# First mixer of a two-network kernel: a third input group takes half of its features early, the recurrence runs two pieces later, and two tables are written in the first feed-forward part

## The reference, cut to what matters

```python
mod = silu(c) @ w_ada + b_ada                  # (2048) @ (2048 x 12288)
sh1, sc1, gt1, sh2, sc2, gt2 = split(mod, 6)
h = rmsnorm(x, g_mix) * (1 + sc1) + sh1
z = h @ w_in                                   # pool | q | k | v | f | x | y
y = concat([pool_mixer(zp), forgetting_attention(zq, zk, zv, zf),
            rg_lru_branch(zx, zy)])
x = x + gt1 * (y @ w_out)
h = rmsnorm(x, g_ffn) * (1 + sc2) + sh2
x = x + gt2 * conv_glu_ffn(h)                  # gate, up, down
```

## Time and profile before

| | |
|---|---|
| median of 3 runs | 3325.72 us |
| profiled execution | 3335.25 us, span 3333.6 us |
| mean granted TensorE clock | 0.976 of full |
| busy share of the span | PE 97%, DVE 67%, ACT 43%, POOL 5% |
| mean DMA rate | 204 GB/s |
| chain that ended last | PE 86%, DVE 7%, DMA 3% |
| first mixer, p = 0 starts | 76.87 us |
| first matmul of quarter 2 (p = 4) | 134.82 us |
| FF1, p = 55 starts | 524.95 us |

### The profile page before, as it was taken

How to read it: one execution, slowest core, us unless ns; L and a number is a source line. 1 busy time by engine, 2 the same in 40 slices (tenths; PEclk the granted TensorE clock), 3 DMA queues, 4 the chain that set the end, 5 groups by cost and what they waited for, 6 DMA issues and landing times.

```text
span 3333.6 us, 62992 instructions
## 1 busy us (share of the span) xinstructions
PE 3221.1 (97%) x27070; PEld 3147.8 (94%) x27070; DVE 2223.1 (67%) x2257; ACT 1420.1 (43%) x1384; POOL 157.7 (5%) x292
## 2 busy tenths in 40 slices
PE   5999979999999999999999999999999999999998
PEld 5988879999999999989999999999988999999998
DVE  5788877766666677677665565567678755555555
ACT  3243334444444444555434433434455443443333
POOL 2111100000000100011000000000011000000000
PEclk7899999999999999999999999999999999999999
DMA  9788776766666745455555555555444555556553
GB/s 385 283 306 314 286 275 222 238 205 202 221 206 202 220 164 159 136 159 166 190 197 189 191 197 190 191 197 168 151 140 157 185 193 197 189 191 197 191 191 137
DMA packets 320747, 681.66 MB, mean 204 GB/s; under 512 B 14768, under 2 KB 21620, under 8 KB 320164
## 3 DMA queue, kind: packets, MB, share of 16 engines
q1 hardware_dynamic: 286272, 562.74, 51.1%
q0 software_dynamic: 31232, 109.07, 9.0%
q10 hardware_dynamic: 3108, 7.89, 0.6%
HBM read 677.47 MB, written 7.94 MB: 206 GB/s over the span
## 4 chain that ended last, share of the span: by engine, by line
PE 86%; DVE 7%; DMA 3%; issue 2%; ACT 1%; POOL 0%; ACTq 0%; DVEq 0%; POOLq 0%; SPq 0%
PE G L695 53%; PE Dn L695 33%; DVE ada_acc L1393 1%; DVE w_lo L1266 1%; PE Dn L698 1%; DMA ada_raw<-in_w_ada 1%; DMA raw<-in_w_in 1%; DMA zT<-in_w_ada 1%; DMA raw<-in_w_out 1%; DVE sq L1317 1%; ACT w_hi L2223 1%; DVE sq L1993 0%; DMA ada_x<-in_w_ada 0%; PE G L698 0%; DVE sq L1333 0%
## 5 line engine op out<-in xcount | busy, mean ns | idle before, releaser
L2223 ACT CAST w_hi<-raw 128x2048 fp32r<-128x2048 f32 (+2 forms) x536 | 1017.5, 1900 | 1418.3 <-DMA raw<-in_w_down 425.6
L1266 DVE TENSOR_TENSOR w_lo<-raw,w_hi 128x2048 fp32r<-128x2048 f32 (+2 forms) x536 | 1218.8, 2274 | 565.1 <-ACT w_hi L2223 564.2
L695 PE MATMUL G<-h_hi,w_hi 128*128 128x256 f32 x5632 | 1579.5, 280 | 13.6 <-DVE w_lo L1266 9.4
L695 PE MATMUL G<-h_lo,w_hi 128*128 128x256 f32 x5632 | 1568.2, 278 | 0.0
L695 PE MATMUL G<-h_hi,w_lo 128*128 128x256 f32 x5632 | 1567.8, 278 | 0.0
L695 PEld LDWEIGHTS G<-h_hi,w_hi 128*128 128x128 f32 x5632 | 1067.7, 190 | 28.6 <-issue 24.4
L695 PEld LDWEIGHTS G<-h_lo,w_hi 128*128 128x128 f32 x5632 | 1067.6, 190 | 0.3
L695 PEld LDWEIGHTS G<-h_hi,w_lo 128*128 128x128 f32 x5632 | 1067.5, 190 | 0.0
L695 PE MATMUL Dn<-act_hi,w_hi 128*128 128x256 f32 x2752 | 763.2, 277 | 7.4 <-DVE act_lo L1811 7.4
L695 PE MATMUL Dn<-act_hi,w_lo 128*128 128x256 f32 x2752 | 762.6, 277 | 0.0
L695 PE MATMUL Dn<-act_lo,w_hi 128*128 128x256 f32 x2752 | 762.5, 277 | 0.0
(11 more groups left out here) (273 smaller groups left out, 1737.4 us busy)
## 6 DMA issues: line engine op xcount, KB each, us to landing
raw<-in_w_up SPq DMA_DIRECT2D x128, 1024.0 KB, 5.4
raw<-in_w_down SPq DMA_DIRECT2D x128, 1024.0 KB, 4.9
raw<-in_w_in SPq DMA_DIRECT2D x88, 1024.0 KB, 5.2
ada_raw<-in_w_ada POOLq DMA_DIRECT2D x120, 512.0 KB, 6.7
raw<-in_w_ffn_gate SPq DMA_DIRECT2D x44, 1024.0 KB, 5.1
raw<-in_w_ffn_up SPq DMA_DIRECT2D x44, 1024.0 KB, 5.2
raw<-in_w_ffn_down SPq DMA_DIRECT2D x44, 1024.0 KB, 5.0
raw<-in_w_o SPq DMA_DIRECT2D x32, 1024.0 KB, 5.0
```

Source lines behind the costliest of these rows:

```text
L695: return nc.tensor.matmul(o, lhsT, rhs, start=start, stop=stop, skip_group_check=True)
L1266: v.tensor_tensor(w_lo[j][:, 0:m], raw[j][:, 0:PIECE_K * n], w_hi[j][:, 0:m], ALU.subtract).then_inc(lo_done, 1)
L2223: s.copy(w_hi[j][:, 0:PIECE_K * n], raw[j][:, 0:PIECE_K * n]).then_inc(hi_done, 1)
```

## The change

A half-filled third group: quarters 0 and 1 of group 2 (the pooling input) become p = 4 and 5, ahead of quarters 2 and 3 of all three groups at p = 6 to 11. Group 2 is gathered in Dn[0] instead of G[0], with a semaphore of its own. The results of the four early blocks of the modulation move to ADA_OUT (two of them to PT). The direct tiles of the last early block are 7, 10, 13 and 15 in place of 2, 5, 8 and 11, and run behind p = 5 in place of p = 3; the third block is closed behind p = 4 and read by DVE there (`second_scale`). The hooks of the small mixers move by two pieces (the convolution by one), the distribution of the 96 later tiles is new, and the temporaries move to the values' tiles of zT. `replicate` is issued by ACT behind pieces 8 to 15 of FF1.

```diff
-ORDER1 = [(0, 0), (0, 1), (1, 0), (1, 1), (0, 2), (0, 3), (1, 2), (1, 3)] + [(g, j) for g in range(2, 9) for j in range(4)]
+HALF1 = [0, 1, 2]
+ORDER1 = [(g, j) for g in HALF1 for j in (0, 1)] \
+    + [(g, j) for g in range(9) for j in ((2, 3) if g in HALF1 else range(4))]
+HALF_AT = 2 * len(HALF1)
+USE1 = {0: (0, 0), 1: (1, 0), 3: (0, 1), 4: (1, 1), 5: (0, 2), 6: (1, 2), 7: (0, 3), 8: (1, 3)}
-ADA_AT = [0, 0, 0, 0, 3, 0, 2, 2, 1, 0, 1, 2, 2, 2, 3, 2, 2, 3, 2, 3, 0, 2, 0, 1, 4, 3, 3, 2, 3, 2,
-          4, 3, 2, 2, 1, 4, 3, 4, 4, 1, 2, 0, 1, 3, 1, 2, 2, 1, 3, 1, 2, 0]
+ADA_AT = [0, 0, 0, 0, 0, 0, 3, 3, 2, 1, 2, 1, 2, 2, 3, 2, 2, 1, 3, 1, 2, 2, 3, 1, 1, 2, 2, 2, 3, 2,
+          2, 1, 3, 2, 3, 2, 1, 3, 2, 3, 2, 3, 2, 3, 2, 3, 2, 3, 2, 2, 2, 0]
-ADA_PE = [[], [3, 6, 9, 12, 15], [3, 8, 13], [2, 5, 8, 11]]
+ADA_PE = [[], [3, 6, 9, 12, 15], [3, 8, 13], [7, 10, 13, 15]]
...
+        ADA_OUT = [Dn[0][:, 0, :], Dn[0][:, 2, :], PT[:, 0, :], PT[:, 1, :]]
+        def group_buf(g):
+            return Dn[0] if g == 2 else G[USE1[g][0]]
...
-            hook(3, ada_total, 2)
+            hook(4, ada_total, 2)
             for t in ADA_PE[3]:
-                hook(3, ada_direct, 3, t)
-            hook(3, ada_total, 3)
+                hook(5, ada_direct, 3, t)
+            hook(5, ada_total, 3)
...
-                hook(11 + b, lru_gates, b)
-            hook(23, pool_map)
+                hook(13 + b, lru_gates, b)
+            hook(25, pool_map)
...
-            hook(2, ada_late, 37, 41)
-            hook(3, second_half)
+            hook(2, ada_late, 37, 40)
+            hook(3, ada_late, 40, 43)
+            hook(4, second_scale)
+            hook(4, ada_late, 43, 46)
+            hook(5, second_half)
...
-            for p, k in ((8, 2), (9, 1), (10, 0)):
+            for p, k in ((9, 2), (10, 1), (11, 0)):
                 hook(p, conv, k)
...
-            hook(22, pool_1)
-            hook(23, pool_2)
+            hook(24, pool_1)
+            hook(25, pool_2)
...
             for q in (2, 3):
-                hook(3, x_hat_hi, q)
+                hook(5, x_hat_hi, q)
             for g in range(len(IN1)):
-                hook(LAST1[g] + 1, evac1, g)
+                hook(LAST1[g] + (0 if g == 0 else 1), evac1, g)
...
-            for n in range(REP):
-                hook(40 + n, replicate, n)
...
+                    if n >= 16 - REP:
+                        replicate(n - 16 + REP)
```

More of the change, by code:

```diff
@@ L795, in ada_direct @@
                     pe.wait_ge(silu_c, 1)
-                    if i >= 2:
-                        pe.wait_ge(mod_ready, i - 1)
+                    if i == 3:
+                        pe.wait_ge(mod_ready, 3)
                 pe.wait_ge(ada_loaded[slot], 16 * count)
                 for j in range(8):
-                    x = mm(ada_out(i)[:, j:j + 1], ada_buf(slot)[:, j * P:(j + 1) * P], c_sil[:, t:t + 1],
+                    x = mm(ADA_OUT[i][:, j:j + 1], ada_buf(slot)[:, j * P:(j + 1) * P], c_sil[:, t:t + 1],
                            t == ADA_PE[i][0] and j == 0, False)
@@ L807, in ada_total @@
                 for j in range(8):
-                    x = mm(ada_out(i)[:, j:j + 1], ada_acc[i % 2][:, j * P:(j + 1) * P], ones[:, 0:1],
+                    x = mm(ADA_OUT[i][:, j:j + 1], ada_acc[i % 2][:, j * P:(j + 1) * P], ones[:, 0:1],
                            not ADA_PE[i] and j == 0, True)
@@ L959, in _ @@
                         misc_open("f")
[L960 to L964, removed]
+                    tiles = [(MISC, 0, True)] + [(buf[:, f, :], 8 + P * f, f % 2 == 0) for f in range(4)]
+                elif j == 0 and g != 2 and USE1[g][1]:
+                    pe.wait_ge(g_free[USE1[g][0]], USE1[g][1])
                 if z0 >= Z_V:
-                    piece_tok(p // 4, p % 4, G[b], 4 * j, j == 0, j == 3)
+                    piece_tok(p // 4, p % 4, buf, 4 * j, j == 0, j == 3)
                 else:
-                    piece(p // 4, p % 4, G[b], h_hi, h_lo, 4 * j, j == 0, j == 3, n, tiles, misc_tile=(g == 0),
+                    piece(p // 4, p % 4, buf, h_hi, h_lo, 4 * j, j == 0, j == 3, n, tiles, misc_tile=(g == 0),
                           call=0 if p == 0 else None)
@@ L972, in _ @@
                 for f in range(4):
-                    b, use = g1_use(len(IN1) + 4 * half + f)
+                    b, use = w_use(4 * half + f)
                     for i, k0 in enumerate(kts):
@@ L1425, in mod_read_first @@
                 dve.wait_ge(ada_sum, i + 1)
-                step(v.tensor_tensor(mod[:, 8 * half:8 * half + 8], Dn[0][:, 2 * (i % 2), 0:8],
+                step(v.tensor_tensor(mod[:, 8 * half:8 * half + 8], ADA_OUT[i][:, 0:8],
                                      cols[:, 8 * half:8 * half + 8], ALU.add))
@@ L1510, in ada_late, with second_scale @@
                 ada_first(lo_, hi_)
-            def second_half():
-                ada_first(41, 46)
+            def second_scale():
                 mod_read_first(2)
@@ L1759, in _ @@
                 for f in range(4):
-                    b, _ = g1_use(len(IN1) + 4 * half + f)
+                    b, _ = w_use(4 * half + f)
                     e = 4 * len(IN1) + 8 * half + 2 * f + 1
```

99 lines of the change are left out of this document (52 added, 47 removed).

## The result

| | before | changed |
|---|---|---|
| median of 7 runs, us | 3325.05 | 3335.53 |
| lowest to highest, us | 3319.77 to 3327.63 | 3332.20 to 3341.69 |
| profiled execution, us | 3335.25 | 3332.20 |
| span of it, us | 3333.6 | 3330.5 |
| ratio to before, 95% interval | | 1.0036 [1.0026, 1.0046] |

The ratio is about 12 us on this kernel, beyond the 0.2% that a measurement tells from no change, and outside the range that was given. The forecast was wrong in its sign.

What follows compares the result with a forecast made beforehand. The mixer, 76.87 to 524.95 us, was taken to decide the time, PE being busy without a break from FF1 on. Gains 2.5 + 7 - 0.5 = 9 us off 3325.7 gave 3316.7 us, range 3304 to 3329.

Steps and rivals of the forecast that it cites:

- The gap: Between third and fourth block closings and quarter 2: two pieces enter, 10.9 us moved, 7.4 us later start, net gain 3.5.
- Behind the gap: Quarter 2 to p = 18: earlier tiles on DVE delay PE about 4 us, spending the 3.5 us gain.
- mostly go: Up to p = 30: two waits for `ada_acc` of 4.5 us mostly vanish, half kept; gain 2.5 us at p = 30.
- p = 30 to 51: Mixer's end: cheaper closings, tables' DMAs gone and fewer `w_lo` waits gain 7 us, bounds 2 and 12.
- worth 2 us: Late mixer: closing of block 8 moves from p = 40 to 43, block 7's from 35 to 37, gaining 2 us.
- the next thing late is DVE: p = 44 to 50: DVE needs 45 us for seven pieces against PE's 38, so DVE limits the gain.
- The tables in FF1: Pieces 8 to 15 of FF1: the copies there cost 0.5 us, mostly hidden because pieces are ready early.
- upper bound of the same paragraph: FF1: if loads grow to 13.3 us as at the mixer's end, waits and restarts cost 9.8 us.
- D: FF1, p = 60 to 70: tables starve the loads, losing 15 us; 3332 to 3336 us in all; chance 0.13.
- C: Mixer: DVE takes it back, start loses 3, tables' gain 2 to 5; 3324 to 3327 us; chance 0.25 with another rival.
- the profile's signs: Expected marks from p = 5 to 55, including p = 30 near 311, p = 55 near 515.5 us, no wait behind it.
- proof of error: Wrong if p = 30 starts later, `w_out` loads take over 12 us, or PE waits for `w_lo` at 580 to 610 us.

Runs made afterwards that it cites:

- second profile of before: The kernel before run once more with no edit: median 3326.08 us, ratio 1.0003, profiled execution 3325.99 us.

## Why the prediction was wrong, by its own steps

**The gap: right.** It said p = 5 ends at 122 to 124 and quarter 2 starts at 140 to 143 us, net gain 3.5; measured 123.5, 142.15 and 3.6. Two small errors cancel in the sum: the direct tiles took 10.3 us for the 11.1 given, since both of the first two ran at full clock, and the two pieces 11.2 for 10.9. DVE's nine tiles were covered, as the sum had them.

**Behind the gap: the step that failed.** It said "I work out about 4 us of delay relative to the gap by p = 18" and "at p = 18 the 3.5 us are spent (-1 to +1)". Measured: 11 us of delay, p = 18 at -7.4. The place (p = 12 and p = 13) and the kind of both waits (`w_lo`, `ada_acc`) were right, and so was the first's size (2.8 us for 3.1). Together they are 6.8 us, beyond the "3 to 6 us together". Three terms of the sum were wrong.

- The two waits were set off against each other: PE's own delay at p = 12 was counted as time in which DVE catches up, so that of 6.5 us of tiles only 1 or so was left as a wait at p = 13. It did not catch up, since its list up to p = 13 was full (16.9 us from the subtraction of p = 12 to the last tile, for PE's 12.9 in p = 12 and 13); the second wait is 4.0, and the two add, to 6.8 us.
- The closing is read by DVE before the gates may open `MISC`, and its reading stood behind a subtraction, the forget sum and a `gelu` step. That is 2.97 us. The reading is one instruction of 0.15 us; it was put down as costing nothing because the instruction costs nothing. The earlier trace rows already had such a reading, of a block in the gap, where nothing stands ahead of it on DVE; behind the gap I should have asked what stands in DVE's order between the last tile and the reading.
- 0.8 us more for the closing (2.60 instead of 1.84) and slower matmuls on either side of it.

For p = 30 the forecast was a gain of 2.5 with a lower bound of -3, and the result -6.9. The bound took the delay as 6 at most and so was no bound. That the waits of the earlier trace rows would "mostly go" is right: no wait for `ada_acc` is left between 238 and 318 us, but `pool_map` waits 2.3 us for `pool_2` in their place, as the same paragraph feared, and from p = 18 to 30 the change wins 0.5 us. The experiment with fewer tiles early (ratio 1.0004 for 1.0036) and the one with early tiles alone (1.0026 for 1) show that this step, and not the order of pieces, is the first cause.

**p = 30 to 51: right in sum, not in its parts.** 7 us were forecast, bounds 2 and 12. From p = 30 to p = 55 the change wins 7.8 us, 7.1 of it behind p = 44, where the waits for `w_lo` are gone. Of the closings I had said that their move is "worth 2 us". Block 8's is: its gap and restart cost 5.9 us over a plain piece before p = 41 in the second profile of before, and 3.9 before p = 44 in the change. Block 7's gives 1.7 back, since it left a wait that stays. The stretch from p = 44 to 51 took 44.5 us for the 45 to 47 given, where the second profile of before has 51.8. What PE still waits for there is DVE's last tile, 2.79 us, as "the next thing late is DVE" had it; the second profile of before has the same 2.79 (the first 1.35).

**The tables in FF1: wrong.** "I take 0.5" became 9.2 (11.0 on the old order). The upper bound of the same paragraph, 9.8, held for the change, though not on the old order; it came from the rows at the mixer's end, where the same copies had done the same harm. The reason for leaving it was that FF1 asks for one piece and one tile per 5.44 us, but what was under way in FF1 beside them is a block of `zpad` too, and the DMA share rose from 0.82 to 0.87. I had put a rule of the page "DMA: Bandwidth & Descriptors" (Arbitration) of the Trainium skill beside it, that engines take turns by whole packets, and worked out from it an estimate, that a load would be late by 1.75 us at most. The trace does not bear the estimate out: the loads' median went from 5.2 to 14.0 us, 9 us late for a pair or two under way. Whether the rule fails here or my use of it is not shown: I took what the profile counts as packets for what the rule calls so. Nor do the pairs come one per piece as I had spread them. The timeline of ACT in the changed kernel has no pair from 569.7 to 583.0 us, while a rounding waits 7.86 us for the late load, and then two within 1.8 us:

```profile
582.99 0.49 ACTq L2312 DMA_DIRECT2D t_rep<-t_row  x1
583.51 0.62 ACTq L2314 DMA_DIRECT2D rpb_rep<-rpb_row  x1
...
584.19 0.49 ACTq L2312 DMA_DIRECT2D t_rep<-t_row  x1
584.71 0.62 ACTq L2314 DMA_DIRECT2D rpb_rep<-rpb_row  x1
```

**The rivals.** D said the tables starve FF1 from p = 60 to 70, at 15 us, and that the time is 3332 to 3336. The time is there and so is the mechanism, but it had a chance of 0.13, its price is 9 us, and by itself it only cancels the mixer's end; a kernel that has it alone is level (1.0001). C said that DVE takes the start's gain back and a little more, to -3 us net, and that the tables' gain shrinks to 2 to 5; the start stood at -7.4 at p = 18, and the mixer's end gave 7.8. That the measured time lies in D's 3332 to 3336 is luck: D had gains of 5 to 9 in front and a loss of 15 in FF1, and what came is a start that loses and 9 in FF1. The result has C's mechanism, larger, and D's, smaller, at once. I had held them for alternatives, and they are at two places that share nothing, so both could come.

What of the profile's signs was right: p5's end, quarter 2's start, both waits at p = 12 and 13 (not their sum), `w_lo` waits under 2 us at the mixer's end, `w_out` loads under 12 us. What it named as proof of error came true twice: p = 30 starts later than before, and PE waits for `w_lo` at 580 to 610 us.

**What stays open.** What the copies do to a load in the DMA engines was not tried by itself. The runs on the early tiles move two things together, how many tiles DVE has before the gates and at which piece block 4 closes; how the 10 us part between the two was not told apart. That the end of FF1 is harmless is shown; whether that is for want of the `zpad` loads or because more pieces are ready there was not told apart.

## What to carry to other kernels

Where work is brought forward onto an engine that has no idle time, count the list up to the point where its result falls due, and count the reader of the result as well: a read of 0.15 us behind 5 us of other work is a 3 us wait for whoever needs the bank. Waits at successive places of a full engine add; none is made up until the engine has idle time, and behind a stall it may idle for want of what the stall delayed. When large copies harm the loads in one place, price them in the next place by the same rows, and look for a place where the loads have nothing else beside them.

## What the runs showed of the hardware

- Single runs of one unchanged kernel lie up to 0.45% apart (3318.4 to 3333.5 us in 12), all on one core. A profiled execution can be any of them: the first of before was 10 us above its median, and had fallen 4.7 us behind the second by p = 55 and 6.2 by p = 72. One profile against one profile would have called this change faster by 3 us.
- Copies from DRAM to DRAM of 0.7 MB a pair lengthen a 1 MB load on another queue from 5.2 to 14.0 us in FF1 (median, 560 to 600 us; DMA share 0.86 without them and 0.95 with them) and from 7.2 to 13.8 at the mixer's end (380 to 530 us, the kernel before without and with its tables there).
- The granted clock in the direct tiles: behind p = 5 the first two, of 16 matmuls of one column each, took 1.84 and 1.93 us, the next two 6.97 together. The granted clock is 1.00 from 123.34 to 125.05 us, 0.96 to 126.98 and 0.50 to 133.66: it fell from the upper (2.4 GHz) to the lower level (1.2 GHz) although PE had no idle time in between.
